# A second mask row on partition 64, and a causal mask matmul in float32r

## The chip, the cores and the metric

The kernel runs on one core of a Trainium2 chip. The metric is the device time of one execution in microseconds, from launch to end. The engines are PE (TensorE, the matmuls; PEld is its weight load), DVE (VectorE), ACT (ScalarE), POOL (GpSimd) and SP (SyncE, which issues the DMAs). TensorE's clock is granted at one of two levels, 2.4 GHz (1.0 in the tables) or 1.2 GHz (0.5).

## The reference

Two transformer blocks over 512 tokens of width 1024, everything in float32. The first has a retention layer and a differential-attention layer. The second puts 16 meta tokens in front and has a feed-forward layer, a mixer of MLA attention beside a gated delta net, and a second feed-forward layer. What matters here are the two masked softmaxes:

```
# differential attention: 8 heads, two halves t of 64 dims, chunks of 64 tokens
mask = key_chunk[None, :] <= q_chunk[:, None]
sc = einsum('bqhtd,bkhtd->bhtqk', q_i, kf) * scale
p = softmax(where(mask, sc, neg))
w = p[:, :, 0] - lam * p[:, :, 1]
out = einsum('bhqk,bkhe->bqhe', w, vf)

# MLA attention: 8 heads, 64 + 32 dims, 16 meta tokens + 512, causal by token
causal = k_pos[None, :] <= q_pos[:, None]
p = softmax(where(causal, s, -inf))
out = einsum('bhqk,bkhd->bqhd', p, v)
```

## The kernel before

The program is one long list for each engine, ordered by hand, with semaphores between the lists. It goes through its stages in turn: projections (weights are loaded as float32, split by ACT and POOL into a high and a low float32r part, and multiplied in three float32r products for each block of 128), retention, the differential attention, feed-forward, the MLA attention, the gated delta net, and so on. Two of the stages have a mask that TensorE adds to the scores.

*The differential attention* (the loop over `s` in `range(ITEMS + HEAD_LAG)`). An item is one head `h` and one block `b` of 128 queries; there are 8 x 4 = 32, four to a head, and block `b` has 128 (b + 1) keys. For each item PE computes the scores of both halves `t` with 64 contracted rows: half 0 lies on partitions 0 to 63, half 1 on 64 to 127, and each goes to a PSUM bank of its own. Masking is a matmul with one contracted row: `ROWS` holds on partition 0 a row of 64 ones and 64 zeros (the stationary operand) and a row of 64 values of -2^100 (the moving one), and their product is added to the last 64 columns of the scores, so that the first 64 queries don't see the last chunk of keys. It is done once for each half, and the second one releases `da_s`, on which VectorE waits with its maximum over both banks (`neg_max`, L1517). ACT then takes the exponentials (`diff_exp`, L1005), DVE combines the halves (`diff_w`, L1536), PE transposes the item before last (`ident,diff_w`, L1977), ACT copies it (`diff_wt`, L1016), and PE multiplies with V (`diff_v,diff_wt`) one item later. PE may write the scores of item s once the exponentials of item s - 2 are done (`da_e`). Once per head the output is normalized (`diff_norm`, L1544 and L1555, with the root on POOL) and transposed by PE (`ident,diff_norm`).

*The MLA attention* (the loop over `s` in `range(HEADS * NT + MLA_LAG)`). Again 32 items. For each, PE computes the scores (96 contracted rows, float32, one matmul or two for the last block) and adds the mask with `mm(o, IDENT, CMASK)`: the identity times a 128x128 tile of zeros and -2^100, both float32, over the last 128 columns. It releases `ma_s`, on which VectorE's maximum waits (L1697; L1700 for the widest block). ACT takes the exponentials (L1157), PE transposes the item before last, ACT copies (`mla_pt`), and PE multiplies with V (`mla_v,mla_pt`).

`mm` (L1974) and `turn` (L1977) are helpers, so that all matmuls have line 1974 in the profile and all transpositions L1977; the tiles tell them apart. Tiles of type float32r are shown as f32 in the matmul rows. A float32 matmul leaves two records in the trace, each with its weight load; a float32r matmul (the projections, the mask rows) leaves one; a transposition leaves one.

`ROWS` is filled at the very start by three memsets on GpSimd (L725 to L727), and `CMASK` comes by DMA (L690) long before its use.

Of the kernel before, what the change touches and what calls it, by code (L numbers as in the profile page):

```python
# [11 lines left out]
F32R = mybir.dt.float32r  # L12
# [5 lines left out]
P = 128  # L18
# [82 lines left out]
def build(nc, A, out):  # L101
    ctx = ExitStack()
    with ctx:
# [7 lines left out]
        def place(name, shape, after, dt=F32, over=None):  # L111

            size = (int(np.prod(shape[1:])) * 4 + 31) // 32 * 32
            at = ends[after] if over is None else starts[over]
            assert at + size <= LAST, (name, at + size - LAST)
            starts[name], ends[name] = at, at + size
            return nc.alloc_sbuf_tensor_at(name, list(shape), dt, offset=at)
# [7 lines left out]
        IDENT = place("ident", [P, P], "w_lo")  # L125
# [17 lines left out]
        ESUM2 = place("exp_sum2", [P, 4, NT], "neg_max2")  # L143
        RSUM2 = place("inv_sum2", [P, 4, NT], "exp_sum2")
        SEL = place("head_rows", [P, 8], "inv_sum2")
        ROWS = place("mask_rows", [1, 256], "head_rows", F32R)
        arena = "mask_rows"


# [1822 lines left out]
        def _(pe):  # L1972
            def mm(o, a, b, start=True, stop=True, **kw):
                return nc.tensor.matmul(o, a, b, start=start, stop=stop, **kw)  # L1974
# [164 lines left out]
            for s in range(ITEMS + HEAD_LAG):  # L2139
                if s < 4 * HEADS:  # L2140
                    h, b = s // NT, s % NT
                    n = P * (b + 1)
                    if s >= 2:
                        pe.wait_ge(da_e, 2 * (s - 1))
                    for t in range(2):
                        r = slice(64 * t, 64 * t + 64)
                        o = PS[:, 2 * (s % 2) + t, :]
                        mm(o[:, 0:n], DQK[r, h, P * b:P * (b + 1)], DQK[r, HEADS + h, 0:n], start=True, stop=False)
                    for t in range(2):
                        o = PS[:, 2 * (s % 2) + t, :]  # L2150
                        last = mm(o[:, n - 64:n], ROWS[:, 0:P], ROWS[:, P:P + 64], start=False, stop=True)
                    last.then_inc(da_s, 1)
                for kind, g in [x for x in (("item", s - 2), ("head", (s - HEAD_LAG) / NT)) if x in turn_no]:
                    g = int(g)
                    no = turn_no[kind, g]
                    if no >= 2:
                        pe.wait_ge(da_wt, no - 1)
                    if kind == "item":
                        pe.wait_ge(da_w, g + 1)
                        for c in range(g % NT + 1):  # L2160
                            last = turn(PS[:, 4 + no % 2, P * c:P * (c + 1)], DW[:, g % 2, P * c:P * (c + 1)], P)
                    else:
                        pe.wait_ge(da_on, 2 * g + 2)
                        for c in range(NT):
                            last = turn(PS[:, 4 + no % 2, P * c:P * (c + 1)], DON[:, g % 2, c, :], P)
                    last.then_inc(da_t, 1)
                if 3 <= s <= ITEMS + 2:
                    g = s - 3
                    h, b = g // NT, g % NT
                    pe.wait_ge(da_wt, turn_no["item", g] + 1)  # L2170
                    if b == 0 and h >= 2:
                        pe.wait_ge(da_on, 2 * (h - 2) + 1)
                    for c in range(b + 1):
                        last = mm(PS[:, 6 + h % 2, P * b:P * (b + 1)], DWT[:, g % 2, P * c:P * (c + 1)],
                                  DV[:, c, P * h:P * (h + 1)], start=c == 0, stop=c == b)
                    last.then_inc(da_pv, 1)
# [72 lines left out]
            for s in range(HEADS * NT + MLA_LAG):  # L2249
                if s < HEADS * NT:  # L2250
                    h, b = s // NT, s % NT
                    n = META + P * (b + 1)
                    if s >= 2:
                        pe.wait_ge(ma_e, s - 1)
                    k = 2 * (s % 2)
                    q = QC[0:R, h, P * b:P * (b + 1)]
                    if n <= 512:
                        mm(PS[:, k, 0:n], q, KCAT[0:R, h, 0:n], start=True, stop=False)
                        o = PS[:, k, n - P:n]
                    else:  # L2260
                        mm(PS[:, k, 0:HALF], q, KCAT[0:R, h, 0:HALF])
                        mm(PS[:, k + 1, 0:HALF], q, KCAT[0:R, h, HALF:TOK], start=True, stop=False)
                        o = PS[:, k + 1, HALF - P:HALF]

                    mm(o, IDENT[:, :], CMASK[:, :], start=False, stop=True).then_inc(ma_s, 1)
                for kind, g in mla_step_turns(s):
                    no = mla_turn_no[kind, g]
                    if no >= 2:
                        pe.wait_ge(ma_pt, no - 1)
                    if kind == "item":  # L2270
                        b = g % NT
                        pe.wait_ge(ma_e, g + 1)
                        for c in range(b + 1):
                            turn(PS[:, 4 + no % 2, P * c:P * (c + 1)], ME[:, g % 3, META + P * c:META + P * (c + 1)], P)
                        if b < NT - 1:
                            o = PS[0:META, 4 + no % 2, P * (b + 1):P * (b + 2)]
                        else:
                            if g >= NT:
                                pe.wait_ge(ma_pt, mla_turn_no["item", g - NT] + 1)
                            o = PS[0:META, 7, 0:P]  # L2280
                        last = turn(o, ME[:, g % 3, 0:META], P)
                    else:
                        pe.wait_ge(ma_on, 2 * g + 2)
                        for c in range(NT):
                            last = turn(PS[:, 4 + no % 2, P * c:P * (c + 1)], MON[:, g % 2, c, :], P)
                    last.then_inc(ma_t, 1)
                if 3 <= s <= HEADS * NT + 2:
                    g = s - 3
                    h, b = g // NT, g % NT
                    pe.wait_ge(ma_pt, mla_turn_no["item", g] + 1)  # L2290
                    if b == 0 and h:
                        pe.wait_ge(ma_on, h)
                    o = PS[:, 6, 64 * b:64 * (b + 1)]
                    hv = slice(64 * h, 64 * h + 64)
                    for c in range(b + 1):
                        mm(o, MPT[:, g % 2, P * c:P * (c + 1)], MV[:, 1 + c, hv], start=c == 0, stop=False)
                    mm(o, MPT[0:META, g % 2, P * (b + 1):P * (b + 2)], MV[0:META, 0, hv],
                       start=False, stop=True).then_inc(ma_pv, 1)
# [217 lines left out]
```

## Time and profile before

| | us |
|---|---|
| median of three timed runs | 2484.56 |
| lowest and highest of them | 2462.92, 2510.17 |
| the profiled execution's own time | 2502.88 |
| its span, first to last instruction | 2501.0 |
| PE busy | 2268.4 (91%) |
| PE weight loads busy | 1955.6 (78%) |
| DVE, ACT, POOL busy | 741.9, 720.8, 769.3 |
| mean granted clock of TensorE | 0.902 |

The profiled execution is one sample. Its 1.9 us beside the span is what lies before the first and after the last instruction. PE's durations are modelled from the start of a matmul and overlap each other, so what one matmul costs in a row of them is read from the distance between starts, not from its duration.

### The profile page before, as it was taken

What the parts mean: (1) busy time and instruction counts of PE and PEld (TensorE: products, weight loads), DVE (VectorE), ACT (ScalarE), POOL (GpSimd) and SP (SyncE); (2) the same over time, 40 slices, a digit from 0 to 9 for tenths busy, and PEclk for the clock granted to TensorE, in tenths of its full rate; (3) what the DMA queues carried; (4) which work ended last, traced back from release to release, by engine and by line L of the source; (5) the groups of instructions that cost most, each with busy time, mean ns of one, the idle gap of its engine ahead of it and who ended that gap; (6) DMA issues with size and microseconds to landing.
All of it is one profiled execution on the core that took longest, in us unless ns stands there. A gap on an engine that the chain in (4) does not pass through costs nothing.

```text
span 2501.0 us, 31700 instructions
## 1 busy us (share of the span) xinstructions
PE 2268.4 (91%) x13215; PEld 1955.6 (78%) x13215; DVE 741.9 (30%) x1262; ACT 720.8 (29%) x1026; POOL 769.3 (31%) x227
## 2 busy tenths in 40 slices
PE   6999899899889899999977999687778998999997
PEld 4898788688657699999965789576666886888886
DVE  4403440333573321001134134234443124110112
ACT  4321232254553222122234333200012223332221
POOL 2442244243113233443431022401111433344432
PEclk8999999799799799999988688768767998999998
DMA  5222123122102122232331012100001232323221
GB/s 163 92 94 76 42 85 101 59 85 85 34 1 84 51 77 79 84 109 71 88 85 34 1 43 68 34 1 1 1 1 34 84 101 68 98 66 121 94 65 44
DMA packets 166995, 162.76 MB, mean 65 GB/s; under 512 B 16476, under 2 KB 164312, under 8 KB 166888
## 3 DMA queue, kind: packets, MB, share of 16 engines
q1 hardware_dynamic: 165736, 159.15, 20.1%
q10 hardware_dynamic: 1152, 2.10, 0.3%
q8 instruction: 78, 1.28, 0.2%
q14 instruction: 29, 0.24, 0.0%
HBM read 159.14 MB, written 2.10 MB: 64 GB/s over the span
## 4 chain that ended last, share of the span: by engine, by line
PE 83%; DVE 6%; issue 5%; ACT 3%; POOL 2%; DMA 0%; POOLq 0%; SPq 0%; DVEq 0%; ACTq 0%
PE ps L1974 80%; PE ps L1977 3%; POOL w_lo L739 1%; DVE tmp L1353 1%; ACT w_hi L848 1%; DVE u_lo L1347 0%; DMA meta_rows<-in_meta_tokens 0%; POOL stat L753 0%; DVE neg_max L1517 0%; DVE gdn_nk L1808 0%; ACT gdn_rows L1226 0%; DVE gdn_vn L1875 0%; DVE gdn_qg L1808 0%; DVE gdn_nq L1808 0%; DVE diag L1330 0%
## 5 line engine op out<-in xcount | busy, mean ns | idle before, releaser
L739 POOL TENSOR_TENSOR w_lo<-w_raw,w_hi 128x2048 fp32r<-128x2048 f32 (+2 forms) x156 | 683.1, 4379 | 1035.0 <-ACT w_hi L848 1035.0
L1974 PE MATMUL ps<-u_hi,w_hi 128*128 128x512 f32 (+1 forms) x1904 | 583.4, 346 | 27.9 <-DVE u_lo L1347 14.4
L1974 PE MATMUL ps<-u_lo,w_hi 128*128 128x512 f32 (+1 forms) x1904 | 583.0, 346 | 0.0
L1974 PE MATMUL ps<-u_hi,w_lo 128*128 128x512 f32 (+1 forms) x1904 | 579.8, 344 | 0.0
L1974 PEld LDWEIGHTS ps<-u_hi,w_hi 128*128 128x128 f32 x1904 | 333.6, 191 | 83.0 <-issue 25.2
L1974 PEld LDWEIGHTS ps<-u_lo,w_hi 128*128 128x128 f32 x1904 | 333.0, 191 | 43.5
L1974 PEld LDWEIGHTS ps<-u_hi,w_lo 128*128 128x128 f32 x1904 | 332.9, 191 | 43.5
L848 ACT ACTIVATE w_hi<-w_raw 128x2048 fp32r<-128x2048 f32 (+2 forms) x156 | 283.3, 1816 | 178.6 <-PE ps L1974 172.8
L1607 DVE TENSOR_TENSOR tmp<-sg,ps 128x528 f32<-128x528 f32 (+1 forms) x44 | 30.6, 696 | 398.5 <-PE ps L1974 398.5
L1974 PE MATMUL ps<-hidden_hi,w_hi 128*128 128x264 f32 (+1 forms) x528 | 141.1, 321 | 0.0
L1974 PE MATMUL ps<-hidden_lo,w_hi 128*128 128x264 f32 (+1 forms) x528 | 140.9, 321 | 0.0
L1974 PE MATMUL ps<-hidden_hi,w_lo 128*128 128x264 f32 (+1 forms) x528 | 140.8, 321 | 0.0
L1974 PE MATMUL ps<-w_lo,u_hi 128*128 128x256 f32 x384 | 107.9, 281 | 0.0
L1974 PE MATMUL ps<-w_hi,u_lo 128*128 128x256 f32 x384 | 107.9, 281 | 0.0
L1974 PE MATMUL ps<-w_hi,u_hi 128*128 128x256 f32 x384 | 107.5, 280 | 0.0
L1974 PEld LDWEIGHTS ps<-hidden_lo,w_hi 128*128 128x128 f32 x528 | 87.8, 188 | 8.1
L1974 PEld LDWEIGHTS ps<-hidden_hi,w_lo 128*128 128x128 f32 x528 | 87.6, 188 | 7.7
L1974 PEld LDWEIGHTS ps<-hidden_hi,w_hi 128*128 128x128 f32 x528 | 87.4, 188 | 8.0
L1081 ACT ACTIVATE hidden_hi<-tmp 128x512 f32 (+3 forms) x44 | 28.2, 640 | 204.1 <-DVE tmp L1607 204.1
L1626 DVE SCALAR_TENSOR_TENSOR residual<-ps,residual 128x528 f32 (+2 forms) x32 | 22.4, 700 | 213.1 <-PE ps L1974 213.1
L1974 PEld LDWEIGHTS ps<-w_hi,u_lo 128*128 128x128 f32 x384 | 72.4, 188 | 0.0
L1974 PEld LDWEIGHTS ps<-w_hi,u_hi 128*128 128x128 f32 x384 | 72.1, 188 | 0.1
(356 smaller groups left out, 3168.6 us busy)
## 6 DMA issues: line engine op xcount, KB each, us to landing
w_raw<-in_w_in_a SPq DMA_DIRECT2D x24, 1024.0 KB, 5.2
w_raw<-in_ffn_w_gate SPq DMA_DIRECT2D x22, 1024.0 KB, 5.4
w_raw<-in_ffn_w_up SPq DMA_DIRECT2D x22, 1024.0 KB, 5.3
w_raw<-in_w_in SPq DMA_DIRECT2D x17, 1024.0 KB, 5.1
w_raw<-in_ffn_w_down SPq DMA_DIRECT2D x16, 768.0 KB, 4.2
w_raw<-in_ffn_w_down SPq DMA_DIRECT2D x16, 640.0 KB, 3.9
w_raw<-in_w_out_a SPq DMA_DIRECT2D x8, 1024.0 KB, 5.0
w_raw<-in_w_kv SPq DMA_DIRECT2D x8, 1024.0 KB, 5.2
```

Source lines behind the costliest of these rows:

```text
L739: pool.tensor_tensor(WL[:, u % SPLITS, 0:size], RAW[:, u % RAWS, 0:size], WH[:, u % SPLITS, 0:size].bitcast(F32), ALU.subtract).then_inc(l ...
L848: nc.scalar.activation(WH[:, u % SPLITS, 0:size], RAW[:, u % RAWS, 0:size], ACT.Copy).then_inc(hi_done, 1)
L1081: nc.scalar.activation(HH[:, bass.ds(4 * i + n, 1), 0:width], TMP[:, m:m + 1, 0:width], ACT.Copy).then_inc(hh_done, 1)
L1353: nc.vector.scalar_tensor_tensor(out=halves(TMP[:, k % 2, 0:width]), in0=halves(x[:, k, cols]), scalar=GAINS[:, gain + k:gain + k + 1], in ...
L1607: nc.vector.tensor_tensor(halves(TMP[:, m, 0:width]), halves(SG[:, m, 0:width]), acc(slot, width), ALU.mult).then_inc(ps_free[slot], 1)
L1626: nc.vector.scalar_tensor_tensor(out=res_chunk(k, cols), in0=acc(slot, width), scalar=0.5, in1=res_chunk(k, cols), op0=ALU.mult, op1=ALU.a ...
L1974: return nc.tensor.matmul(o, a, b, start=start, stop=stop, **kw)
L1977: return nc.tensor.transpose(o, x, IDENT[0:n, 0:n])
```

## The change

`ROWS` gets 128 partitions in place of one, so the three memsets write the same rows on every partition, and the mask matmul of half `t` reads partition 64 `t`: 0 for half 0 and 64 for half 1. The tile takes as many bytes of a partition as before. The causal mask matmul reads identity and mask as float32r instead of float32.

```diff
-        ROWS = place("mask_rows", [1, 256], "head_rows", F32R)
+        ROWS = place("mask_rows", [P, 256], "head_rows", F32R)
...
                     for t in range(2):
                         o = PS[:, 2 * (s % 2) + t, :]
-                        last = mm(o[:, n - 64:n], ROWS[:, 0:P], ROWS[:, P:P + 64], start=False, stop=True)
+                        r = slice(64 * t, 64 * t + 1)
+                        last = mm(o[:, n - 64:n], ROWS[r, 0:P], ROWS[r, P:P + 64], start=False, stop=True)
                     last.then_inc(da_s, 1)
...
-                    mm(o, IDENT[:, :], CMASK[:, :], start=False, stop=True).then_inc(ma_s, 1)
+                    mm(o, IDENT[:, :].bitcast(F32R), CMASK[:, :].bitcast(F32R), start=False, stop=True).then_inc(ma_s, 1)
```

## Rows read from the trace of the kernel before

**Rows 1.** The page: TensorE's busy time, and the granted clock in 40 slices.
```profile
PE 2268.4 (91%) x13215; PEld 1955.6 (78%) x13215; DVE 741.9 (30%) x1262; ACT 720.8 (29%) x1026; POOL 769.3 (31%) x227
...
PEclk8999999799799799999988688768767998999998
```

**Rows 2.** Both attention loops: window, length, busy us (x instructions) by engine, clock, DMA.
```profile
core 0: us, PE busy (x) PEld busy (x) DVE busy (x) ACT busy (x) POOL busy (x), PEclk, DMA share, GB/s
649.00:738.00 89.00, 81.72 (x429) 55.97 (x430) 61.29 (x146) 49.17 (x165) 6.04 (x6) 0.81 0.00 1
...
1352.50:1455.50 103.00, 96.23 (x447) 81.28 (x447) 19.07 (x45) 34.73 (x100) 0.00 (x0) 0.70 0.00 1
```

**Rows 3.** Chain of work in the differential loop: start, us, what, records merged.
```profile
710.21 1.68 PE ps L1974 x10
...
712.47 1.85 PE ps L1974 x12
...
715.08 2.30 PE ps L1974 x14
```

**Rows 4.** Chain of work in the MLA loop.
```profile
1407.84 2.67 PE ps L1974 x12
```

**Rows 5.** Waits in the MLA loop: in total, times, the longest.
```profile
DVE neg_max L1697 <- PE ps L1974: 75.5, 24, 12.1
```

**Rows 6.** The tile of mask rows: count, ns min/median/max, first and last start.
```profile
L1974 PE MATMUL ps<-mask_rows x64: 271/292/416, 649.5 to 737.5; 1*128 1x64 f32 x64
```

**Rows 7.** Timeline of PE at clock 1.0: start, us, operation, records merged.
```profile
712.87 0.28 PE L1974 MATMUL ps<-diff_v,diff_wt 128*128 128x128 f32 x1
713.07 0.59 PE L1974 MATMUL ps<-diff_qk 64*128 64x384 f32 x2
...
713.50 0.49 PE L1974 MATMUL ps<-diff_qk 64*128 64x384 f32 x2
713.92 0.29 PE L1974 MATMUL ps<-mask_rows 1*128 1x64 f32 x1
...
714.05 0.27 PE L1974 MATMUL ps<-mask_rows 1*128 1x64 f32 x1
714.26 0.33 PE L1977 MATMUL ps<-ident,diff_w 128*128 128x128 f32 x1
```

**Rows 8.** Timeline of PE at clock 0.5: the two mask matmuls of one item.
```profile
691.73 0.42 PE L1974 MATMUL ps<-mask_rows 1*128 1x64 f32 x1
...
691.96 0.40 PE L1974 MATMUL ps<-mask_rows 1*128 1x64 f32 x1
```

**Rows 9.** Timeline of the same head: VectorE, and the head's transposition on PE.
```profile
713.46 0.68 DVE L1555 TENSOR_TENSOR diff_norm<-diff_norm,rstd 128x512 f32<-128x512 f32 x1
...
714.36 0.96 DVE L1517 TENSOR_REDUCE neg_max<-ps 128x2 f32<-128x768 f32 x1 [0.22 <-PE ps L1974]
...
714.42 0.66 PE L1977 MATMUL ps<-ident,diff_norm 128*128 128x128 f32 x4
...
717.40 1.23 DVE L1517 TENSOR_REDUCE neg_max<-ps 128x2 f32<-128x1024 f32 x1 [1.23 <-PE ps L1974]
```

**Rows 10.** Timeline of PE in the MLA loop, at clock 1.0, then 0.5.
```profile
1440.27 0.28 PE L1974 MATMUL ps<-causal,ident 128*128 128x128 f32 x1
...
1440.49 0.27 PE L1977 MATMUL ps<-ident,mla_exp 128*128 128x128 f32 x1
...
1402.30 0.42 PE L1974 MATMUL ps<-causal,ident 128*128 128x128 f32 x1
...
1402.72 0.42 PE L1977 MATMUL ps<-ident,mla_exp 128*128 128x128 f32 x1
...
1403.58 0.31 PE L1974 MATMUL ps<-mla_v,mla_pt 128*128 128x64 f32 x1
```

**Rows 11.** Stretch of float32r projections with 256 moving columns, columns as in the loops' table.
```profile
190.00:200.00 10.00, 10.00 (x87) 10.00 (x87) 0.00 (x0) 3.00 (x3) 3.98 (x1) 1.00 0.32 105
```

**Rows 12.** Single heads: two of the differential loop, one of the MLA loop.
```profile
699.98:710.21 10.23, 9.02 (x59) 6.32 (x59) 8.45 (x21) 6.71 (x23) 1.01 (x1) 1.00 0.01 2
...
685.18:699.98 14.80, 13.60 (x58) 9.71 (x58) 8.54 (x21) 6.70 (x23) 1.01 (x1) 0.65 0.00 0
...
1381.80:1400.40 18.60, 17.86 (x64) 14.89 (x64) 2.54 (x6) 5.06 (x16) 0.00 (x0) 0.50 0.00 0
```

## Prediction

> **What bounds the kernel now.** I read the page's busy shares and clock slices first. PE is busy for 91% of the span, and its granted clock moves between its two levels, 2.4 GHz and 1.2 GHz [rows 1]. So a PE instruction is worth its full spacing wherever nothing else is late, and about double where the clock is at 1.2 GHz. The change touches two PE loops alone, so next I read the table by stretch. The differential attention lasts 89 us with the clock at 0.81. The causal (MLA) attention lasts 103 us at 0.70 [rows 2]. Together they are 192 us, 8% of the span. All that the change can move directly is PE time inside them.
>
> Then the chain of work in each. In the differential loop one head takes 10.2 us at full clock. Its chain is PE without a break from the first P·V product after a copy to the last mask of the head, in pieces of 10, 12 and 14 records of L1974 [rows 3]. Each piece is V products, 4 score records and 2 mask records (4+4+2, 6+4+2, 8+4+2). VectorE's maximum, the exponentials and a copy follow, and then the next piece. So the mask pairs of key blocks 1, 2 and 3 stand on the chain. The pair of block 0 runs while VectorE is working on block 3, and is off it, except in the first head. In the causal loop the chain is PE too, in pieces that hold V products, scores and the mask [rows 4], and VectorE waits for PE there 75.5 us in 24 waits [rows 5].
>
> **Part 1: the second mask row on partition 64.** The scores use partitions 0 to 63 for half 0 and 64 to 127 for half 1, and the timeline shows what that does. Both score matmuls of a pass start within 0.01 us of each other (713.07, x2), and the second passes stand 0.43 us later. The two mask matmuls, both on partition 0, start 0.13 us apart at full clock (713.92, 714.05). Then the next transposition comes 0.21 us after the second [rows 7]. At half clock the two are 0.23 us apart [rows 8]. There are 64 of them, with one load each [rows 6]. After the change they should start together like the score pair, so a pair gives back 0.13 - 0.01 = 0.12 us at full clock and 0.23 - 0.01 = 0.22 us at half.
>
> Of the 32 pairs, 23 show the short spacing and 9 the long one. Eight belong to block 0. One of these, the loop's first (long), is on the chain, one is long and off it, and six are short and off it. That leaves 17 short and 8 long pairs: 17 x 0.12 + 8 x 0.22 = 2.0 + 1.8 = 3.8 us.
>
> Is another engine late when PE comes earlier? In a head at full clock PE gains 0.12 at block 1, 0.24 by block 2 and 0.36 by block 3. VectorE sits idle 0.22 us before the maximum of block 2 and 1.23 us before that of block 3. Block 3 is where the chain leaves PE, so 0.36 fits. The head turn on PE (714.42) reads what VectorE's L1555 ends at 713.46 + 0.68 = 714.14, a slack of 0.28 against a shift of 0.24 [rows 9]. It holds, narrowly. If it did not, some 0.05 us would go in each of five heads, which I leave in the range. Bounds of this part: none of the 0.12 comes (0 us), or moving from one group of rows to another costs a pause. The only pause that the rows show is that at the change from 128 rows to 64: 712.87 to 713.07 is 0.20 us, where the spacing before it is 0.11, so 0.09. Once per pair on the chain that is 25 x 0.09 = 2.3 us lost, against 25 x 0.12 = 3.0 given back at full clock alone. I take the score pair's behaviour, as it is the same engine, the same two row groups and the same two banks a few hundred ns earlier. The two pauses around the mask pair stay as they are.
>
> The Trainium skill's "TensorEngine Tiling (Array Packing)", section "Instruction Overhead", says that each matmul has an overhead of some 60 cycles and that a narrow matmul costs no less. By it the second mask matmul would be worth about 25 ns at 2.4 GHz, and the part 25 x 0.025 = 0.6 us (an estimate from that page). The 0.13 us between the two mask starts does not agree: this matmul is dearer than that [rows 7].
>
> The three memsets that fill the rows now write 128 partitions. They are POOL's first work, 650 us before their reader, and no wait is added anywhere; no tile behind the rows moves, since the tile keeps its 1,024 bytes a partition. Nothing for this.
>
> **Part 2: the causal mask as float32r.** Today this matmul is float32 and leaves two records, each with its own weight load, 32 x 2 = 64. At full clock the first starts at 1440.27 and the next operation at 1440.49: 0.22 us. At half clock it is 1402.30 to 1402.72: 0.42 us [rows 10]. As float32r it should leave one record and one load, as the mask rows do (64 matmuls, 64 records) [rows 6]. What that one pass of 128 columns costs the trace does not show, and two rows bound it.
> - Low end: the float32r projections of 256 columns run 87 matmuls in 10.0 us, 0.115 us each [rows 11]. If 128 columns stream at that rate, the pass hides behind its weight load, which keeps the spacing of a narrow pass at 0.11 (half of the 0.22 above). Saved: 0.11 us at full clock and 0.42 - 0.11 = 0.31 at half.
> - High end: the float32r mask rows have 64 columns, and at half clock one lasts 0.42 us [rows 8]. That is what a 128-column float32 pass lasts (0.42); a 64-column float32 pass lasts 0.31 [rows 10]. So a narrow float32r column costs twice a float32 pass's column, and one float32r pass as much as the two float32 passes that it replaces. Saved: nothing but a load that is hidden already.
>
> I take the high end: 64 columns is nearer to 128 (64 away) than 256 is (128 away), and it is a lone small matmul between float32 work, like this one. So 0 us, with 6.5 us as the other end: 17 items at full clock and 15 at or into half clock give 17 x 0.11 + 15 x 0.31 = 1.9 + 4.7 = 6.5 (after rounding). A loss I exclude up to rounding: the pass would have to outlast two float32 passes, which is beyond either row. In that loop nothing but PE would be late: VectorE waits for it.
>
> The Trainium skill's "TensorE: Matmul & The Clock Gate", section "Back-to-back issue gap", gives N/2.4 + 2.5 ns at full clock. By it 128 columns would take 56 ns, the weight load would be the limit, and the sum would be that of the low end. The mask rows' spacing of 0.13 us for 64 columns speaks against the formula for narrow float32r.
>
> **Sum.** The profiled execution took 2502.9 us (span 2501.0); less 3.8 it would be 2499.1. It lies 18 us above the median of the three timed runs, 2484.6, so the forecast is 2484.6 - 3.8 = 2480.8, and I say 2481.
>
> **Rivals.**
> A. The one pass streams at the projections' rate: 3.8 + 6.5 = 10.3 us, 2474. For it: 256 columns do. Against it: 64 columns do not.
> B. The second mask row is not run beside the first. For it: one contracted row is a smaller group than the scores' 64, and no row shows two such matmuls in different groups. Against it: the score pair. Then 2484.6, or 2487 with a pause.
> C. Slower, through the clock. PE gets fewer records in a loop where the granted clock is already at 1.2 GHz for 60% of the time, and the level there could stay low. A head wholly at half clock takes 18.6 us [rows 12]. Seven such follow one another in the 103 us stretch: 7 x 18.6 = 130, 27 us more, less 3.8, which gives 2508. It decides once the stretch's clock falls from 0.70 to below about 0.67, where 103 x 0.70 / 0.67 - 103 = 4.6 us are lost. The same in the differential loop: a head takes 10.2 us at 1.00 and 14.8 at 0.65 [rows 12], or (14.8 - 10.2)/0.35 = 13 us per unit of clock; 8 heads from 0.81 to 0.50 are 8 x 13 x 0.31 = 32 us. Only both together, 55 us net, pass 2%. Against it: the engine stays busy to the same share, and nothing is made to wait.
>
> **How the numbers follow.** Forecast 0.52; A 0.25; B 0.15; C 0.08. The cases lie within 2474 and 2508, and the three runs of one kernel already lie within 2463 and 2510, 22 below and 26 above their median. That spread is wider than all terms of the sum, so the range takes it in: 2456 (case A less most of the lower spread) to 2508 (case C, or the forecast with the upper spread). Two per cent, about what a measurement of this kernel can tell from no change, is 50 us; no case reaches it on the fast side, and on the slow side only C at its fullest. Faster 0.015, same 0.97, slower 0.015.
>
> **What the profile will show.** Mask pairs starting together instead of 0.13 or 0.23 us apart, and full-clock heads of the differential loop at about 9.86 us in place of 10.22. One record of the causal mask per item, 32 in all, with 0.21 to 0.22 us (full) or 0.42 (half) from it to the next operation; 0.11 there means A. Mask pairs still 0.13 apart mean B. A clock in the causal stretch under 0.67 means C, provided that several executions show it. The prediction is wrong if a stretch that the change does not touch moves by more than these terms, most likely through the level of the clock.

## The result, and the profile after

The changed kernel takes 2507.1 us (median of 20 executions, 2489.0 to 2517.3), the kernel before 2490.3 us (median of 20; 19 lie within 2462.9 and 2515.7, and a single one of 3705.6 us counts in nothing below but this median). The ratio is 1.0091 with a 95% interval of 1.0060 to 1.0122. It leaves out every execution more than 1.5% above the fastest of its own kernel, which here takes out five slow ones of before and none of the changed kernel, since that has no execution under 2489 us; so it overstates the loss. The means of all executions are 15.2 us apart (plus or minus 8.6 at 95%), and 16.7 us with the further executions of before used below. That is clear of noise, though under the 2% bound. The forecast was 3.8 us faster.

The profiled execution of the changed kernel has a span of 2500.5 us, as good as the 2501.0 of the one before. So two profiles alone show no loss, and the comparison has to go stretch by stretch. First the page, with what answers to [rows 1].

```profile
PE 2271.0 (91%) x13183; PEld 1952.8 (78%) x13183; DVE 742.4 (30%) x1262; ACT 720.8 (29%) x1026; POOL 769.2 (31%) x227
```

There are 32 records and 32 loads fewer, and PE is busy no less. Then both loops by stretch, to be set against [rows 2]. The columns are the window, its length, busy us (and instructions) by engine, the granted clock, and DMA.

```profile
651.40:739.70 88.30, 80.41 (x423) 53.70 (x425) 61.33 (x145) 48.29 (x162) 6.04 (x6) 0.77 0.00 1
1353.60:1459.80 106.20, 100.00 (x418) 82.56 (x419) 18.68 (x43) 36.33 (x102) 0.00 (x0) 0.61 0.02 6
```

The MLA loop has less work and takes 3 us more (106.2 against 103.0), at a clock of 0.61 instead of 0.70. The differential loop is level, at 0.77 instead of 0.81. Now the instructions themselves: the mask pair at full clock, for [rows 7], and the causal mask at full and at half clock, for [rows 10].

```profile
712.64 0.49 PE L1974 MATMUL ps<-diff_qk 64*128 64x384 f32 x2
713.06 0.30 PE L1974 MATMUL ps<-mask_rows 1*128 1x64 f32 x2
713.28 0.33 PE L1977 MATMUL ps<-ident,diff_w 128*128 128x128 f32 x1
...
1365.55 0.61 PE L1974 MATMUL ps<-mla_k,mla_q 96*128 96x264 f32 x2
1365.80 0.42 PE L1974 MATMUL ps<-causal,ident 128*128 128x128 f32 x1
1366.05 0.28 PE L1977 MATMUL ps<-ident,mla_exp 128*128 128x128 f32 x1
...
1381.66 1.09 PE L1974 MATMUL ps<-mla_k,mla_q 96*128 96x264 f32 x2
1382.18 0.68 PE L1974 MATMUL ps<-causal,ident 128*128 128x128 f32 x1
1382.66 0.41 PE L1977 MATMUL ps<-ident,mla_exp 128*128 128x128 f32 x1
```

The two masks now form one piece (x2) of 0.30 us, and the transposition follows 0.22 us after its start, where before it was 0.34 us (713.92 to 714.26). The causal mask is one record. Its row starts as soon as the last score pass has been started, so the 0.25 us to the next operation hold that pass too, and the mask has to be read together with it. The last two score passes begin at 1365.55, and the transposition comes 0.50 us later. The same two passes in the kernel before:

```profile
1439.83 0.61 PE L1974 MATMUL ps<-mla_k,mla_q 96*128 96x264 f32 x2
```

There the transposition comes at 1440.49 [rows 10], 0.66 us later. So 0.16 us went, and of the 0.22 us that the mask took, 0.06 are left. The prediction's sign for this (0.21 to 0.22 us from the record to the next operation for its high end, 0.11 for rival A) would have misled: the 0.25 us here look like the high end, because they hold the score pass. Both instructions got cheaper. What got dearer is the rest of the MLA loop, more of which ran at 1.2 GHz.

### The profile page after: what moved, and what is told of

It is laid out like the page before. It is cut to its first block, busy times and chain, and to the rows that moved or that the text cites. A ratio compares the mean times of both kernels' runs of the same rounds, so it can differ in the third digit from the quotient of the medians.

```text
span 2500.5 us, 31636 instructions
## 1 busy us (share of the span) xinstructions
PE 2271.0 (91%) x13183; PEld 1952.8 (78%) x13183; DVE 742.4 (30%) x1262; ACT 720.8 (29%) x1026; POOL 769.2 (31%) x227
## 4 chain that ended last, share of the span: by engine, by line
PE 83%; DVE 6%; issue 5%; ACT 3%; POOL 2%; DMA 0%; POOLq 0%; SPq 0%; DVEq 0%; ACTq 0%
PE ps L1974 80%; PE ps L1977 3%; POOL w_lo L739 1%; DVE tmp L1353 1%; ACT w_hi L848 1%; DVE u_lo L1347 0%; DMA meta_rows<-in_meta_tokens 0%; POOL stat L753 0%; DVE gdn_nk L1808 0%; ACT gdn_rows L1226 0%; DVE gdn_vn L1875 0%; DVE gdn_qg L1808 0%; DVE gdn_nq L1808 0%; DVE diag L1330 0%; ACT sq L860 0%
```

## The experiments

All numbers are from the chip. "Ratio" is against the kernel before on the same chip, with its 95% interval, and formed as in the result: it comes out up to 0.6% above the ratio of the means of all executions, so the means stand beside it. "Loop" is read in the profiled execution, from the first to the last score matmul.

### Which part loses?

E1 is the kernel before once more, without an edit.

> The kernel of before, unchanged, to get more of its executions with their clocks and a second profile. Both theories expect a ratio of 1.000. Clock theory (the granted clock costs what the instructions give back): the times of single executions follow their mean granted clock, about 25 us for each 0.010 of it; in the profile the MLA stretch has a clock near 0.70 and the differential one near 0.81, as in the first profile. Chance theory (the first profile of before and the timed runs differ by where the clock happened to stand): the clock of the MLA stretch differs by 0.05 or more between the two profiles of the same kernel.

Measured: ratio 1.0016 [0.9978, 1.0054], 2487.1 us. The second profile shows the same program with both loops 29 us shorter together, for [rows 2]:

```profile
649.40:731.90 82.50, 75.17 (x425) 51.54 (x425) 60.96 (x145) 48.46 (x163) 6.05 (x6) 0.88 0.00 1
1344.00:1424.80 80.80, 73.78 (x450) 62.93 (x451) 18.70 (x43) 35.10 (x102) 0.00 (x0) 0.94 0.02 5
```

This is the row that my prediction lacked. The MLA loop of one kernel takes 80.8 us at 0.94 or 103.0 us at 0.70. The clock theory's guess of a stable level fell; its other half, that an execution's time follows its mean clock, held (below). The chance theory is right about *one execution* and says nothing of a mean. With this run and the runs of before beside the other experiments, on four chips, there are 107 executions of the unchanged program with their mean clocks (seven more on a fifth chip would not move what follows). A line through them gives 21.9 us for each 0.010 of the clock, so 2190 us for a whole unit, and they lie about it with a spread (standard deviation) of 1.6 us. Mean 2489.0 us at 0.908. So a kernel can be judged twice: by its time, and by its time against that line, which estimates its work at equal clock.

E2, the mask rows alone (the causal mask is float32 again):

```diff
-                    mm(o, IDENT[:, :].bitcast(F32R), CMASK[:, :].bitcast(F32R), start=False, stop=True).then_inc(ma_s, 1)
+                    mm(o, IDENT[:, :], CMASK[:, :], start=False, stop=True).then_inc(ma_s, 1)
```

> The mask rows of the differential attention on partitions 0 and 64 alone; the causal mask stays float32. Theory A (the loss comes from the causal mask: PE streams less in the MLA loop and its clock there falls): 3 us faster than before, ratio 0.999, MLA stretch at about 0.70 as before. Theory B (the loss comes from the mask rows: the paired masks lower the clock in the differential loop): slower, ratio 1.004 to 1.009, clock of the stretch 649 to 760 us at or under 0.76, MLA stretch as before. Theory C (part 1 and part 2 share it): 1.002 to 1.005.

E3, the float32r mask alone (`ROWS` as in the kernel before).

> The causal mask as float32r alone; both mask rows stay on partition 0. Theory A: ratio 1.007 to 1.012, mean granted clock of an execution 0.01 lower than that of before, MLA stretch at 0.64 or less although each item needs 0.16 us (full clock) or 0.31 us (half) less. Theory B: 7 us faster, ratio 0.997, with the clock of before. Theory C: 1.002 to 1.005.

| | executions | mean us | mean clock | against the line | ratio |
|---|---|---|---|---|---|
| before | 107 | 2489.0 | 0.908 | 0 | |
| E2 rows only | 12 | 2483.0 | 0.909 | -3.6 | 0.9999 [0.9955, 1.0043] |
| E3 float32r only | 12 | 2503.7 | 0.899 | -5.2 | 1.0090 [1.0050, 1.0130] |
| both (the change) | 20 | 2505.7 | 0.896 | -8.9 | 1.0091 [1.0060, 1.0122] |

The float32r mask alone has the whole loss. In means it is 13.0 us slower than before on the same chip (plus or minus 6.9), the rows alone 7.7 us faster (plus or minus 9.0). At equal clock the float32r mask is 5.2 us faster, and its clock takes 0.009 x 2190 = 20 us. The work saved by the two parts adds up (3.6 + 5.2 = 8.8 against 8.9), and for the change the books close: 0.0117 x 2190 = 25.6 us lost, 8.9 gained, 16.7 slower, the difference of the means. In the profile of E3 the MLA loop is at half clock nearly throughout, and its waits are those of [rows 5] (77.4 us in 24 here):

```profile
1343.60:1456.50 112.90, 107.01 (x419) 87.61 (x420) 18.70 (x43) 36.37 (x102) 0.00 (x0) 0.57 0.01 4
...
1389.70:1406.20 16.50, 15.71 (x58) 12.78 (x56) 2.52 (x7) 4.53 (x13) 0.00 (x0) 0.50 0.01 1
1406.20:1423.60 17.40, 16.61 (x62) 13.64 (x60) 2.57 (x7) 5.12 (x14) 0.00 (x0) 0.50 0.00 0
```

Every second head also holds the transposition of a finished pair of heads and is longer. Such a head at half clock takes 17.4 us where it took 18.6 [rows 12]: 1.2 us less for four items, 0.30 us each, or 0.32 between the starts of the heads' first score matmuls (18.65 to 17.37). A pass at the projections' rate would save 0.31. Theory A holds for the loss; theories B and C fall.

### Is it the streaming that holds the clock?

E4 and E5 put work back that changes nothing in the output: a float32r matmul of 384 columns into the bank of the scores, just before the scores overwrite it. E4 adds it to the changed kernel, E5 to E3, E6 to the kernel before. E7 adds two of 512 columns to E3. E8 is the control: one float32 matmul of *one* column in the same place of E3. That is two records and two loads for each item, where the change took away one of each (482 records in the loop, against 450 with the float32 mask and 419 without), so it puts back twice what was gone.

```diff
                     q = QC[0:R, h, P * b:P * (b + 1)]
+                    mm(PS[:, k, 0:3 * P], IDENT[:, :].bitcast(F32R),
+                       CMASK[:, :].bitcast(F32R).unsqueeze(1).to_broadcast([P, 3, P]))      # E4, E5, E6
+                    mm(PS[:, k, 0:1], IDENT[:, :], CMASK[:, 0:1])                           # E8
```

> The changed kernel with one more float32r matmul of 384 zero or -2^100 columns per MLA item, written into the scores' bank just before the scores overwrite it; the result does not depend on it. With the mask's own 128 columns that is 512 float32r columns an item, as long as the two float32 passes of before (0.21 us at full clock). Theory A in the form that streaming sets the level: the clock of the MLA stretch comes back to 0.70 or more, mean clock up by 0.01 against the changed kernel, and the time goes to 0.998 to 1.002 of before although 32 matmuls were added. If float32 columns count for more than float32r ones, or if the clock is not the cause: the stretch stays at 0.64 and the time is the changed kernel's plus 5 to 10 us, ratio 1.011 to 1.013.

> The causal mask as float32r alone, plus one float32r matmul of 384 columns per MLA item into the scores' bank before the scores overwrite it. Streaming theory (the MLA loop keeps its clock when PE streams as much as with the float32 mask): the distribution of before comes back, ratio 0.997 to 1.003 with some executions near 2465 us, MLA stretch at 0.70 to 0.94. Rival (the mask's type or the weight loads decide, not the streaming): ratio 1.010 to 1.014, stretch at 0.54 to 0.64.

> The kernel before, float32 mask and all, plus the same 384-column matmul per MLA item: 32 more matmuls in a loop that PE bounds. Streaming theory: all executions now have the MLA stretch at 0.90 or more, which takes 81 us at full clock (second profile of before) plus 5 for the added work in place of 103, so the median falls to 2470 to 2478 us, ratio 0.992 to 0.996. Rival (work added to the bounding engine costs its time): 5 to 10 us slower, ratio 1.002 to 1.004.

> The float32r mask, plus two float32r matmuls of 512 columns per MLA item, one into each bank of the scores. Streaming theory: MLA stretch at 0.95 or more in every execution; 32 x 2 x 0.21 = 14 us of added work at full clock on a loop of 81 less 5: 90 us against 103 or 113. Ratio 0.994 to 0.999. Rival: 14 to 28 us slower than the float32r mask alone, ratio 1.015 to 1.020.

> The float32r mask, plus one float32 matmul of one column per MLA item: two weight loads and two records, as many as the change took away, but hardly any column streamed. Streaming theory: the clock stays low, MLA stretch 0.54 to 0.64, and the added work makes it 3 to 7 us slower than the float32r mask alone: ratio 1.009 to 1.013. If the number of matmul instructions or weight loads keeps the clock up: ratio 0.998 to 1.003, stretch 0.70 or more.

| | ratio | mean us | mean clock | against the line | MLA loop, us | its clock |
|---|---|---|---|---|---|---|
| E4 the change, 384 columns more | 1.0045 [1.0012, 1.0079] | 2493.5 | 0.905 | -1.8 | 96.9 | 0.75 |
| E5 float32r, 384 more | 1.0060 [1.0012, 1.0109] | 2498.4 | 0.904 | +0.9 | 103.2 | 0.70 |
| E6 float32 mask, 384 more | 1.0039 [0.9997, 1.0081] | 2493.0 | 0.908 | +5.2 | 94.4 | 0.84 |
| E7 float32r, 2 x 512 more | 1.0058 [1.0015, 1.0100] | 2492.2 | 0.911 | +9.0 | 104.5 | 0.79 |
| E8 float32r, one column | 1.0177 [1.0102, 1.0253] | 2520.9 | 0.895 | +3.7 | 120.4 | 0.59 |

With columns the loop's clock comes back to 0.70 or more in the profiles, and over all executions it rises from 0.896 to 0.905 (E4 against the change) and from 0.899 to 0.904 and 0.911 (E5 and E7 against E3). E4 has a lower median (2493.5 us) than the changed kernel although it does more. With loads and records alone the clock does not come back. But the forecasts of E6 and E7, full clock in every execution, missed; the ratios of E4, E5 and E8 lie above their ranges, though those of the means (1.001, 1.002 and 1.011) lie within; and the ratio of E6 is the one that its rival gave (1.002 to 1.004). E6 is the plainest miss: the same columns that raised the clock of E4 and E5 left that of the float32 kernel where it was (0.908 before and after). With one profile of each and a loop that can do either, this is not enough to settle it. So I made the loop longer.

E9 to E12 run the MLA loop four times over, the same eight heads again, with the same output. (`MHD = 4 * HEADS` takes the place of `HEADS` in the bounds of the loop on PE, ACT and DVE, and `h % HEADS` that of `h` in the operands.) E9 has the float32 mask, E10 float32r, E11 float32r with the matmul of 384 columns, E12 float32r with that of one column.

> The kernel before with the MLA loop run four times over (128 items in place of 32, the same heads again, the same output), so that one profile shows 32 heads instead of 8. Streaming theory: the loop goes back and forth between the two clock levels, mean clock 0.70 to 0.95 over all four passes, 325 to 410 us (81 to 103 a pass). Chance theory (the loop's clock is set by where it starts, not by its work): all four passes at one level, and which one differs between executions.

> The same four passes with the float32r mask. Streaming theory: at half clock throughout or nearly, mean 0.50 to 0.62, 430 to 455 us (106 to 113 a pass), so this kernel is 40 to 120 us slower than the one with four float32 passes. Chance theory: the same mixture of levels as with float32, and 4 x 5 to 10 us = 20 to 40 us faster than it.

> Four passes, float32r mask plus a 384-column float32r matmul an item (512 float32r columns with the mask, as long as the two float32 passes). Streaming theory: clock and time of the float32 version within 0.05 and 20 us. Rival (type or records decide): the clock of the float32r version, and 128 x 0.16 to 0.32 = 20 to 40 us more than it.

> Four passes, float32r mask plus a one-column float32 matmul an item: two loads and two records, nearly nothing streamed. Streaming theory: at half clock throughout as the float32r version, and 128 x 0.22 = 28 us slower than it. If records or loads decide: back to the float32 version's clock, 0.70 or more.

Medians: 2827.0, 2891.0, 2782.4 and 2944.1 us. The lowest and highest executions of E9 (2807, 2836), E10 (2888, 2893) and E12 (2941, 2957) don't touch each other. E11 lies at 2777 to 2790, but for the profiled one at 2829, the longest of its five. The loops in the profiles, one row each of E9, E10, E11 and E12:

```profile
1343.80:1780.10 436.30, 405.86 (x1938) 343.37 (x1939) 79.69 (x187) 149.00 (x426) 0.00 (x0) 0.71 0.01 1
```
```profile
1343.50:1846.90 503.40, 477.52 (x1812) 391.95 (x1812) 79.68 (x187) 152.02 (x426) 0.00 (x0) 0.54 0.00 1
```
```profile
1359.90:1787.50 427.60, 397.57 (x1938) 335.35 (x1938) 79.66 (x187) 147.50 (x426) 0.00 (x0) 0.73 0.01 2
```
```profile
1351.40:1899.90 548.50, 522.56 (x2067) 438.56 (x2067) 79.66 (x187) 151.54 (x426) 0.00 (x0) 0.55 0.00 1
```

With float32 the heads change levels again and again (of the 31 whole ones 7 at full clock, 10 at half, the rest across a change). With float32r 25 of the 31 are at half clock. The chance theory falls: the work of the loop decides how often it is at full clock, and where it starts only colours the beginning. That the float32r type of the mask by itself, or the number of records, holds the clock down is out too (E11, E12). How much the float32 passes count for is not settled. E11, forecast within 20 us of E9, is 45 us faster by the medians, at a mean clock of the executions of 0.898 against 0.884, with a fill made to last as long as those passes. E9 was longer than expected (436 us against at most 410) and E10 too (503 against 455): both ranges were four times a single pass, and a single pass has its first one or two heads at full clock for free. E12 is 53 us slower than E10, twice the 28 expected, since its added passes run at half clock too.

### Does the other loop do the same?

E13 and E14 run the differential loop four times over in the same way, with the mask rows of before and of the change. (The copy of a finished head goes to a scratch tile in the first three passes, since its place holds queries that are needed again.)

> The kernel before with the differential attention run four times over (32 heads, same output). The profiles so far show one pass at 82 us with clock 0.88, 88 at 0.81 and 102 at 0.68. Both theories expect a mixture of levels: 330 to 400 us for four passes.

> The same four passes with the mask rows on partitions 0 and 64. Arithmetic theory: 3 pairs a head are on the chain, each 0.11 us cheaper at full clock and 0.21 at half by the rows of the changed kernel, so 32 x 3 x 0.11 to 0.21 = 11 to 20 us faster than the four passes of before, at the same mean clock of the loop within 0.02. Clock theory: PE streams less here too, the loop's clock falls by 0.03 or more, and the kernel is no faster or up to 30 us slower.

Inconclusive as a whole. Four executions each: E13 2712, 2713, 2812 and 2824 us (loop in the profile 327.9 us at 0.97), E14 2739 to 2767 (360.7 us at 0.84). E13's executions lie in two pairs, E14's between them, and the means, 2765 and 2753, are 12 us apart, within that spread. The mean clocks of the four executions are the same too, 0.904 and 0.904; against a line through E13's four, E14's lie 7 to 13 us lower, some 10 us of work saved (an estimate from eight executions).

The profiles of all experiments say more on the clock. Eleven show a single pass of this loop with both mask rows on partition 0 and no fill in it. Six of them have five of the seven whole heads at full clock, one after another, two have three (before, E12), and E5, E6 and E11 lie at a clock of 0.68 to 0.73; E13 has 29 of 31. Five show it with the pair and no fill (the change, E2, E4, E17, E18). None has more than one head at full clock, and E14 has 10 of 31, every third. The mean clock of the loop is 0.82 with the one and 0.77 with the other, its mean length 88.2 and 89.7 us. So in these profiles, few as they are, the pair too gives back in clock what it saves; the mean clock of E2's executions (0.909 against 0.908) does not show it.

What the profiles do settle is a head at full clock: 10.23 us with both masks on partition 0, 10.12 with the pair. That is 0.11 us saved and not 0.36. At half clock it is more: the first head, at half clock in the profiles of before and after, went from 9.16 to 8.34 us, 0.21 for each of its four pairs. The first head of before and of after, then a later one of after at full clock, for [rows 12]:

```profile
648.75:657.91 9.16, 9.16 (x29) 5.00 (x29) 4.42 (x10) 3.22 (x13) 0.00 (x0) 0.50 0.00 0
```
```profile
651.40:659.74 8.34, 8.34 (x30) 4.18 (x30) 4.43 (x10) 3.22 (x13) 0.00 (x0) 0.50 0.00 0
706.90:717.02 10.12, 8.75 (x59) 5.88 (x58) 8.45 (x21) 6.71 (x22) 1.01 (x1) 1.00 0.00 1
```

Why so little at full clock? VectorE in such a head of before, and then of E14, in which lines are one higher (start, us, instruction, and the idle time before it where there was any), against [rows 9]:

```profile
711.34 0.68 DVE L1549 TENSOR_REDUCE ssq<-diff_sq 128x4 f32<-128x512 f32 x1
...
712.13 0.69 DVE L1517 TENSOR_REDUCE neg_max<-ps 128x2 f32<-128x512 f32 x1
```

```profile
834.65 0.75 DVE L1537 SCALAR_TENSOR_TENSOR diff_w<-diff_exp,coef 128x512 f32<-128x512 f32 x1
835.32 0.68 DVE L1550 TENSOR_REDUCE ssq<-diff_sq 128x4 f32<-128x512 f32 x1
836.04 0.17 DVE L1552 TENSOR_SCALAR var_eps<-ssq 128x4 f32<-128x4 f32 x1
836.12 0.69 DVE L1518 TENSOR_REDUCE neg_max<-ps 128x2 f32<-128x512 f32 x1
...
838.13 0.96 DVE L1518 TENSOR_REDUCE neg_max<-ps 128x2 f32<-128x768 f32 x1
...
838.40 0.66 PE L1978 MATMUL ps<-ident,diff_norm 128*128 128x128 f32 x4
...
841.27 1.22 DVE L1518 TENSOR_REDUCE neg_max<-ps 128x2 f32<-128x1024 f32 x1 [1.34 <-PE ps L1975]
```

The maximum of block 1 (836.12) stands behind the sum of squares on VectorE, not behind PE. Nothing idles between them, in the kernel before either. So PE's earlier masks buy nothing there, and the 0.22 us of idle time before block 2 is gone. PE then waits for the copy behind block 1's exponentials, until 838.40.

### Can the clock be had for nothing?

In each head PE stands idle once: 1.1 us in the differential loop, while VectorE finishes `diff_w`, and 1.3 us in the MLA loop, while it normalizes (from one product to the next in the chain below). E15 (rows only) and E16 (the whole change) stream 512 float32r columns twice and three times there, into a bank that is free and overwritten next; the products are used by nobody. E17 keeps those of the MLA loop alone on the changed kernel. E18 is its control: three float32 matmuls of one column in the same place, nearly as long but with next to no columns. In the cut the bank expression of the second part is shortened.

```diff
                     if kind == "item":
+                        if s % NT == 0:
+                            for _ in range(2):
+                                mm(PS[:, 4 + no % 2, :], IDENT[:, :].bitcast(F32R),
+                                   IDENT[:, :].bitcast(F32R).unsqueeze(1).to_broadcast([P, 4, P]))
                         pe.wait_ge(da_w, g + 1)
...
                     if b == 0 and h:
+                        for _ in range(3):
+                            mm(PS[:, <free bank, 4 or 5>, :], IDENT[:, :].bitcast(F32R),
+                               IDENT[:, :].bitcast(F32R).unsqueeze(1).to_broadcast([P, 4, P]))
                         pe.wait_ge(ma_on, h)
```

> Mask rows on two partitions, float32 causal mask, and float32r matmuls of 512 columns put where PE stands idle: two before the transposition that waits for block 3's neighbour in each differential head, three before the wait for the normalized head in each MLA head, into banks that are free and overwritten next. At full clock they take 0.43 and 0.64 us of idle stretches of 1.1 and 1.3 us. If streaming in the idle stretches holds the clock: the MLA loop stays at 0.90 or more in all executions, median 2462 to 2475 us, ratio 0.990 to 0.995. Rival (the level hangs on what stands between these stretches): ratio 0.999 to 1.003, levels as before.

> The changed kernel (mask rows and float32r causal mask) with the same matmuls in PE's idle stretches. If streaming there holds the clock: the float32r mask's 5 to 7 us are kept and the ratio is 0.988 to 0.996. Rival: the MLA loop stays at half clock, ratio 1.006 to 1.012 as for the changed kernel.

> The changed kernel with the three 512-column float32r matmuls before the wait for the normalized head in the MLA loop alone. Streaming theory: MLA loop at full clock, 71 us against 106, and the differential loop as in the changed kernel with 82 to 102 us: median 2462 to 2480 us, ratio 0.990 to 0.998.

> The same places filled with three float32 matmuls of one column each: six records and six weight loads, about 0.66 us at full clock like the three wide ones, but hardly a column streamed. Streaming theory: MLA loop at 0.54 to 0.64 as in the changed kernel, ratio 1.007 to 1.012. If it is enough that PE has work there: ratio 0.990 to 0.998 as for the wide ones.

| | median us | lowest, highest | ratio | mean clock | against the line |
|---|---|---|---|---|---|
| E15 rows, both loops filled | 2457.1 | 2455.7, 2461.7 | 0.9893 [0.9862, 0.9925] | 0.921 | -2.6 |
| E16 the change, both filled | 2453.0 | 2452.2, 2458.1 | 0.9884 [0.9840, 0.9929] | 0.921 | -7.7 |
| E17 the change, MLA filled | 2463.5 | 2460.6, 2468.5 | 0.9945 [0.9913, 0.9977] | 0.915 | -9.0 |
| E18 MLA, one column | 2512.3 | 2487.9, 2517.8 | 1.0136 [1.0079, 1.0192] | 0.896 | -9.1 |

E16 and E17 lie in their ranges. E15 came out faster than its range, E18 slower.

E15's loops first, then E16's:

```profile
649.10:725.60 76.50, 71.77 (x437) 45.79 (x439) 60.88 (x145) 48.66 (x165) 6.04 (x6) 0.96 0.00 1
1338.30:1413.80 75.50, 73.22 (x467) 61.56 (x468) 18.69 (x43) 34.63 (x102) 0.00 (x0) 1.00 0.03 8
```
```profile
649.60:726.10 76.50, 71.77 (x438) 45.80 (x439) 60.86 (x145) 48.66 (x165) 6.04 (x6) 0.96 0.00 1
1338.90:1409.90 71.00, 68.37 (x436) 56.67 (x437) 18.69 (x43) 34.56 (x102) 0.00 (x0) 1.00 0.02 8
```

Here is what the float32r mask is worth when the clock stays: 75.5 - 71.0 = 4.5 us, 0.14 us an item. The chain of E16's MLA loop shows that the added matmuls cost nothing: from the last product of a head (`x15`) to the next head it is a run of VectorE steps, and no added matmul is on it. Nor is a head at full clock longer for them: 10.22 us in E15, 10.28 for the same head in E1.

```profile
1378.40 2.36 PE ps L1974 x15
1380.83 0.59 issue
1381.41 0.18 DVE inv_sum L1708
1381.61 0.43 DVE mla_norm L1714
1382.09 1.30 PE ps L1974 x7
```

E15's and E16's executions agree within 6 us where those of before are over 50 us apart. The wide fill against the narrow one in the same idle stretch, E17 against E18, is 49 us in the medians. At equal clock the two are level with each other and with the change (-9.0, -9.1, -8.9), so neither fill costs anything, and the whole difference is clock: 0.915 against 0.896. Both add three matmuls; the wide ones leave three records and fill 0.95 us, the narrow ones six and fill 0.73 us, which leaves PE idle for 0.31 and 0.45 to 0.57 us. PE's busy share of the loop is the same, 96%. The fill and the loop, E17 first, then E18:

```profile
1383.30 0.95 PE L1974 MATMUL ps<-ident 128*128 128x512 f32 x3
1384.56 0.80 PE L1974 MATMUL ps<-mla_v,mla_pt 128*128 128x64 f32 x4 [0.31 <-DVE mla_norm L1714]
```
```profile
1350.90:1422.00 71.10, 68.42 (x436) 56.73 (x437) 18.69 (x43) 34.63 (x102) 0.00 (x0) 1.00 0.02 6
```
```profile
1369.08 0.73 PE L1974 MATMUL ps<-ident 128*128 128x1 f32 x6
1370.38 0.44 PE L1974 MATMUL ps<-mla_v,mla_pt 128*128 128x64 f32 x2 [0.57 <-DVE mla_norm L1714]
```
```profile
1356.30:1442.60 86.30, 83.25 (x454) 71.56 (x455) 18.68 (x43) 35.76 (x102) 0.00 (x0) 0.80 0.02 7
```

E18's clock was not as low as expected in its profiled execution (0.80 in a loop of 86.3 us), which at 2487.9 us was the shortest of its six; the other five reach to 2517.8. In these loops the matmuls with columns held the clock, and an equal busy share without them did not. That the idle time left over (0.45 to 0.57 against 0.31 us) has a part in it is not excluded by this pair. E16 is the fastest of all: 1.2% faster than before by the ratio, 1.5% by the means, and 54 us faster than the changed kernel.

## Why the prediction was wrong, by its own steps

**The step that failed** is the argument against rival C: "the engine stays busy to the same share, and nothing is made to wait". Both halves were true (PE is busy for 94% of the MLA loop, 100.0 of 106.2 us, against 93% before) and neither kept the clock up: over all executions it fell from 0.908 to 0.896. The sum held the granted clock constant and priced the change at it. At that constant clock it was close: 3.6 + 5.2 = 8.9 us measured, against 3.8 to 10.3. What it left out was 25.6 us of clock. Rival C had the clock, the place and nearly the size (2508 us; 2507 measured), and a chance of 0.08. Its cause was not the right one: it named the fewer records, and E8 and E12 put records back, twice as many as were gone, with the clock still low. That its time came out so near is luck in part, since its 27 us of clock stand on a base 4 us too low and against 3.8 us of gain instead of 8.9. Its own number said what to fear, that a fall from 0.70 to 0.67 eats the gain; it fell to 0.61 and 0.57 in the profiles. But the 0.70 was one draw: the same loop of the kernel before stood at 0.94 in E1.

**Part 1, the pairs.** The masks start together, as forecast, and a pair saves the 0.12 us (0.34 to 0.22 in the rows). The 3.8 us came out at 3.6 at equal clock, but by luck and not for the reason given. At full clock a head gives 0.11 us and not 0.36 (10.12 us, where 9.86 was forecast): I looked at the idle time before blocks 2 and 3 and not at block 1, where VectorE has none. More falls at half clock, 0.82 us in the first head.

**Part 2, the float32r mask.** The high end was taken (two float32 passes' worth), and this term of the sum was mis-sized: 0 us, where 5.2 were measured. The low end was nearer: 0.14 us saved an item at full clock (0.16 in the rows) and 0.30 at half, against 0.11 and 0.31 in rival A. At full clock it saved more than A allowed, so the 0.11 us of a weight load was no floor. "64 is nearer than 256" was no argument. The mask rows differ from the causal mask in more than width (one contracted row), and two rows cannot say which of the two makes a column dear. A's 10.3 us are near the 8.9 of work; its 2474 failed for the time, like the main forecast.

**The formula of the Trainium skill** ("TensorE: Matmul & The Clock Gate", section "Back-to-back issue gap") gives 56 ns for the causal mask's 128 columns, and the rows agree: 0.06 us were left of 0.22. I set it aside because of the mask rows. For their 64 columns it gives 29 ns (an estimate by that formula), and 0.13 us were measured, so it doesn't hold for them.

**The base.** The median of three, 2484.6, was that of a few draws from a kernel that lies between 2463 and 2519; 20 executions gave 2490.3. The range, up to 2508, held the median of 2507.1 only just.

**What stays open.** How much pairing the mask rows lowers the clock of the differential loop: the profiles say from 0.82 to 0.77 on average, but E2's time does not show a loss within half a per cent, and E13's executions (2712 or about 2820 us) lie on both sides of E14's. Why the fill inside the items (E4 to E7) holds the clock only in part and does nothing for the float32 kernel (E6), and why that in the idle stretch holds it wholly, was not taken further; the two differ in place, in the number of columns and in the idle time left. So columns are shown to matter, and a count of them alone doesn't tell the clock. Of the two fills in E16, that of the differential loop is worth 2463.5 - 2453.0 = 10.5 us, but it was not run alone, and E17 ran on another chip.

## What to carry to other kernels

Before pricing a saving on TensorE, look at the granted clock of the stretch. If it stands between the two levels, the loop goes back and forth between them, and taking streamed columns out can cost more in clock than it saves, as here (5.2 us saved, 20 lost). One profile does not tell such a loop's clock: it was 0.70 and 0.94 for the same program. Compare kernels at equal mean clock as well as by time; the difference between the two tells work from clock. And where TensorE has an idle stretch once per iteration, try useless wide matmuls in it. Here they cost nothing and were worth 1.2%, more than the optimization they rescued.

## What the runs showed of the hardware

- The same program's MLA loop took 80.8 us at a clock of 0.94 in one execution and 103.0 at 0.70 in another; with the idle stretches filled, 75.5 at 1.00.
- A float32r matmul of 128 columns and 128 contracted rows costs 0.14 us less than the float32 one at full clock (75.5 against 71.0 us for 32 items, E15 and E16) and 0.30 less at half (E3). One of 64 columns with a single contracted row lasts 0.42 us at half clock, no less than a float32 pass of 128 columns.
- Two matmuls of one contracted row on partitions 0 and 64 start within 0.01 us of each other (the change), both on partition 0 0.13 us apart at full clock [rows 7].
- Six matmul records with one column each in PE's idle stretch did not hold the clock (E18, MLA loop at 0.80 in the profile); three records of 512 columns in the same place did (E17, at 1.00), at a busy share of 96% in both.
